# Experts sorted by tokens and run in pairs of 128 and 64 slots, the 64 resting as high and low rows side by side

## The reference, cut to what matters

```python
logits = (xt @ router_w).astype(jnp.float32)          # (256, 8)
top_logit, top_idx = lax.top_k(logits, TOP_K)         # TOP_K = 2
gates = jax.nn.softmax(top_logit, axis=-1)
...
def swiglu(x, w1, w2):
    gate, up = jnp.split(x @ w1, 2, axis=-1)          # w1: 1024 x 5632
    return (jax.nn.silu(gate) * up) @ w2              # w2: 2816 x 1024
...
yb = yb * slot_gate[:, None]
y = jnp.zeros_like(xt).at[slot_tok].add(yb)
```

## Time and profile before

| | us |
|---|---|
| median of 3 runs (1501.88 to 5215.01) | 1502.48 |
| span of the profiled execution | 1499.8 |
| PE busy in it | 1470.4 (98%) |
| DVE busy | 1172.5 (78%) |
| ACT busy | 944.0 (63%) |
| moved from memory | 388.41 MB, mean 259 GB/s |

### The profile page before, as it was taken

The page is one execution under the profiler, slowest core; times in us unless marked ns, Lnnn a source line. Parts: engine busy times, 40 slices in busy tenths (PEclk is TensorE's granted clock), DMA queues, the critical chain, the costliest instruction groups (busy, mean ns, idle before and its releaser), DMA issues.

```text
span 1499.8 us, 21512 instructions
## 1 busy us (share of the span) xinstructions
PE 1470.4 (98%) x8395; PEld 1278.7 (85%) x8395; DVE 1172.5 (78%) x1150; ACT 944.0 (63%) x963; POOL 52.2 (3%) x58
## 2 busy tenths in 40 slices
PE   7999999999999999998999999999999999999997
PEld 7989898999889989897788888888888888888885
DVE  7878655555447878655998988989989899898996
ACT  6655444444437654444777778777787777777774
POOL 0031000000000131000000000000000000000000
PEclk9999999999999999999999999999999999999999
DMA  8443443445546433534799989999999999999994
GB/s 311 141 141 113 168 164 117 169 171 195 181 164 219 141 113 117 193 114 167 282 359 382 347 341 364 352 378 361 340 357 347 380 362 343 361 347 377 365 357 157
DMA packets 54478, 388.41 MB, mean 259 GB/s; under 512 B 6000, under 2 KB 6256, under 8 KB 8176
## 3 DMA queue, kind: packets, MB, share of 16 engines
q1 hardware_dynamic: 53840, 384.98, 68.7%
q10 hardware_dynamic: 544, 2.10, 0.4%
HBM read 386.00 MB, written 1.05 MB: 258 GB/s over the span
## 4 chain that ended last, share of the span: by engine, by line
PE 92%; DVE 3%; DMA 2%; ACT 1%; issue 1%; POOL 0%; SPq 0%; DVEq 0%; ACTq 0%
PE pb L1059 27%; PE pb L1061 27%; PE pb L1060 27%; PE pb L1461 1%; PE pb L1424 1%; PE pb L1207 1%; PE pb L1289 1%; PE pb L1309 1%; DVE xTl L1636 1%; DMA arena<-in_mem 1%; DVE wlo L2177 1%; PE pb L1040 1%; PE pb L1447 0%; PE pb L1448 0%; DMA raw<-in_lin_w 0%
## 5 line engine op out<-in xcount | busy, mean ns | idle before, releaser
L2177 DVE TENSOR_TENSOR wlo<-raw,whi 128x2048 fp32r<-128x2048 f32 x175 | 400.3, 2291 | 47.7 <-ACT whi L961 46.2
L961 ACT ACTIVATE whi<-raw 128x2048 fp32r<-128x2048 f32 x175 | 335.6, 1920 | 131.9 <-PE pb L1061 131.9
L1587 DVE TENSOR_TENSOR wlo<-raw,whi 128x2048 fp32r<-128x2048 f32 (+1 forms) x101 | 226.0, 2246 | 133.2 <-ACT whi L602 133.0
L1059 PE MATMUL pb<-whi,mTh 128*128 128x512 f32 x768 | 305.2, 397 | 1.6 <-DVE wlo L2177 1.6
L1061 PE MATMUL pb<-whi,mTl 128*128 128x512 f32 x768 | 300.1, 391 | 0.0
L602 ACT ACTIVATE whi<-raw 128x2048 fp32r<-128x2048 f32 (+1 forms) x101 | 189.9, 1884 | 172.3 <-PE pb L1061 167.3
L1059 PE MATMUL pb<-xTh,whi 128*128 128x256 f32 x736 | 210.2, 286 | 2.7 <-DVE xTl L1624 1.2
L2177 DVE TENSOR_TENSOR kvXr<-kvX,whi 128x2048 fp32r<-128x2048 f32 x86 | 196.7, 2291 | 19.3 <-ACT whi L961 17.7
L1060 PE MATMUL pb<-xTl,whi 128*128 128x256 f32 x736 | 208.2, 283 | 0.0
L1061 PE MATMUL pb<-xTh,wlo 128*128 128x256 f32 x736 | 208.2, 283 | 0.0
L1060 PE MATMUL pb<-wlo,mTh 128*128 128x512 f32 x528 | 205.6, 389 | 0.0
(11 more groups left out here) (341 smaller groups left out, 2195.4 us busy)
## 6 DMA issues: line engine op xcount, KB each, us to landing
raw<-in_ffn_w SPq DMA_DIRECT2D x209, 1024.0 KB, 4.8
kvX<-in_ffn_w SPq DMA_DIRECT2D x88, 1024.0 KB, 4.9
raw<-in_lin_w SPq DMA_DIRECT2D x64, 1024.0 KB, 4.8
raw<-in_lin_w SPq DMA_DIRECT2D x4, 536.0 KB, 5.6
arena<-in_mem ACTq DMA_DIRECT2D x2, 1024.0 KB, 8.5
h<-in_x SPq DMA_DIRECT2D x1, 1024.0 KB, 4.9
out<-xn SPq DMA_DIRECT2D x2, 512.0 KB, 3.1
consts<-in_con SPq DMA_DIRECT2D x1, 838.0 KB, 13.6
```

What stands on the lines that cost most here:

```text
L961: nc.scalar.activation(whi[:, (MOE0 + c) % HRING, :], xraw_slots[c % XRING], ACT.Copy).then_inc(hi_ready, 1)
L1059: nc.tensor.matmul(o, lh, rh, start=first, stop=False)
L1587: V.tensor_tensor(wlo[:, m % RING, c], raw[:, m % RING, c], whi[:, m % HRING, c].bitcast(F32), ALU.subtract).then_inc(lo_ready, 1)
L2177: V.tensor_tensor(xlo_slots[c % XRING], xraw_slots[c % XRING], whi[:, (MOE0 + c) % HRING, :].bitcast(F32), ALU.subtract).then_inc(lo_ready, 1)
```

## The change

Experts are sorted by their number of tokens and run in four pairs of a full one (H, 128 slots) and a light one (L, 64 slots). The first full one is always expert 0, which needs no sorting; the other seven are ordered by DVE (MAX, MAX_INDEX on 8 x count + index), the three largest become H, the next four L. SP and nobody else needs the ids as registers (`value_load`). For a light expert the 64 high rows and the 64 low rows of the tokens rest side by side as one stationary operand of 128 columns, so a product takes two matmuls (times high weights, times low weights) instead of three, 8 a chunk instead of 12; the upper 64 rows of the result are then added to the lower 64: ACT copies them down (`low_rows`), DVE adds (`lsum`). The two experts of a pair run interleaved by units (a unit: 2 chunks of w1, or 1 of w2; 22 units an expert), L three units behind H. `WHOLE` is empty: every chunk is split. The gate now scales the expert's output where it is split, so both experts of a pair are spread into one sum and added once. The ring of loaded chunks has a seventh slot (`raw6r` in the `arena`). The loops over pairs are unrolled on ACT, DVE, SP and PE. The second pass runs if expert 0 or the largest other has over 128, or the fourth of the others over 64.

```diff
-XRING = 6
+XRING = 7
+PAIRS_E = NE // 2
+UNITS = NF // 2 + W2_CHUNKS
+LAG = 3
+LIGHT = P // 2
+WHOLE = ()
+def turns():
+    total = PAIRS_E * UNITS
+    return [((divmod(a, UNITS) if a < total else None), (divmod(a - LAG, UNITS) if a >= LAG else None))
+            for a in range(total + LAG)]
+STREAM = [(kind, at[0], c) for step in turns() for kind, at in zip("HL", step) if at
+          for c in unit_chunks(at[1])]
...
+        def column(kind, i):
+            return (i - 1) % NE if kind == "H" else NE // 2 - 1 + i
...
             def load_experts(p):
-                with sp.Fori(0, NE // 2) as pair:
-                    for e in range(2):
-                        for c in range(FFN_CHUNKS):
-                            m = e * FFN_CHUNKS + c
-                            sp.wait_ge(w_used, pair * (2 * FFN_CHUNKS) + (moe_chunk(p) + m - XRING + 1))
-                            sp.dma_start(xraw_slots[m % XRING], ffn_w[1 + pair * 2 + e, c]
-                                         ).then_inc(x_loaded[m % XRING], 16)
+                ids = {}
+                for n, (kind, i, c) in enumerate(STREAM):
+                    at = p * NSTREAM + n
+                    if at >= XRING:
+                        sp.wait_ge(w_used, MOE0 + at - XRING + 1)
...
+                    if (kind, i) != ("H", 0) and (kind, i) not in ids:
+                        if len(ids) == 0:
+                            sp.wait_ge(sorted_ok, 1)
+                        q = column(kind, i)
+                        ids[kind, i] = sp.value_load(eid[0:1, q:q + 1].bitcast(U32), min_val=0, max_val=NE - 1)
+                    e = ids.get((kind, i), 0)
+                    slot = landed(p, n)[0]
+                    sp.dma_start(xraw_slots[slot], ffn_w[1 + e, c]).then_inc(x_loaded[slot], 16)
...
+                def first_product(kind, i, j):
...
+                            if kind == "L":
+                                both = xg[:, k, P:2 * P]
+                                nc.tensor.matmul(o, both, w[0][:, kk, :], start=first, stop=False)
+                                mm = nc.tensor.matmul(o, both, w[1][:, kk, :], start=False, stop=last)
...
+                                mm = split_product(o, [xgh[:, k, 0:P], xgHl[:, k, :]],
+                                                   [part[:, kk, :] for part in w], first, last)
+                        mm.then_inc(w_used, 1)
...
+                def turn_light(i, j):
+                    pe.wait_ge(lg_ready, pair_no(p, i, j))
```

More of the change, by code:

```diff
@@ L284, in build @@
+        xlo_slots = [kvXr[:, 0, :], kvXr[:, 1, :]] + [wlo[:, (MOE0 + i) % RING, :] for i in range(RING)] + [
+            over("raw6r", RAW6, CW)]
         raw12 = small_(NT * 12).rearrange("p (t c) -> p t c", c=12)
@@ L923, in experts @@
             def experts(p):
[L924 to L932, removed]
-                        ins.then_inc(xg_hi, 1)
@@ L947, in two_experts @@
[L947 to L989, removed]
+                w = par_("ffn_w", 1)
+                done = [HRING]
+                def splits_through(n):
+                    while done[0] < NSPLIT and SPLIT[done[0] - HRING] <= n:
+                        split_high(p, done[0])
+                        done[0] += 1
@@ L1004, in experts @@
                 return more if p == 0 else None
[L1006 to L1011, removed]
             more = experts(0)
             with act.If(more):
-                for c in range(HRING):
-                    first_chunk(1, c)
+                for i in range(HRING):
+                    split_high(1, i)
                 experts(1)
@@ L1549, in experts @@
                     pe.wait_ge(xn_lo, 2)
-                for phase in range(2):
-                    gather(p * (NE // 2), phase, 6 - 2 * phase)
-                if p == 0:
-                    for pair in range(NE // 2 - 1):
-                        two_experts(pair, False)
-                else:
-                    with pe.Fori(0, NE // 2 - 1) as pair:
-                        two_experts(pair, False)
-                two_experts(NE // 2 - 1, True)
+                gather_first("H")
+                for a, (full, light) in enumerate(turns()):
+                    if full:
+                        i, u = full
+                        if u < NF // 2:
+                            first_product("H", i, u)
+                        else:
+                            second_product("H", i, u - NF // 2).then_inc(w_used, 1)
+                        if 1 <= u <= NF // 2:
+                            turn_hidden(i, u - 1)
+                    if a == 1:
+                        gather_first("L")
+                    if light and not full and light[1] == UNITS - 2:
+                        break
+                    if light:
+                        i, u = light
+                        if u < NF // 2:
+                            first_product("L", i, u)
+                        else:
+                            second_product("L", i, u - NF // 2).then_inc(w_used, 1)
+                        if 1 <= u <= NF // 2:
+                            turn_light(i, u - 1)
+                    if full:
+                        i, u = full
+                        if u in (5, 7) and i:
+                            spread_outputs(i - 1, (u - 5) // 2)
+                        if u == 9:
+                            turn_selections(i)
+                        if u in (15, 18) and i < PAIRS_E - 1:
+                            gather(i + 1, (u - 15) // 3)
@@ new lines, in first_lo_of @@
+            def first_lo_of(p, kind):
+                w = par_("ffn_w", 1)
+                for r in (range(4) if kind == "H" else (4,)):
+                    dve.wait_ge(first_hi, 5 * p + r + 1)
+                    for k in (range(2 * r, 2 * r + 2) if kind == "H" else range(KT)):
+                        if kind == "H":
+                            low, src, s = xgHl, pb[:, 4 + r, (k % 2) * P:(k % 2 + 1) * P], slice(0, P)
+                        else:
+                            low, src, s = xgLl, pb[:, 3, k * LIGHT:(k + 1) * LIGHT], slice(P, XG)
+                        ins = V.scalar_tensor_tensor(out=low[:, k, :], in0=src, scalar=w[:, k:k + 1],
+                                                     in1=xgh[:, k, s].bitcast(F32), op0=ALU.mult, op1=ALU.subtract)
+                    ins.then_inc(first_lo, 1)
@@ new lines, in _ @@
+            select_full([pos[:, t, 0:1] for t in range(NT)]).then_inc(sel_ready, 1)
+            split_low(0, 1)
+            first_lo_of(0, "H")
+            split_low(0, 2)
+            dve.wait_ge(rt_rank, 2)
+            counts = pb[:, 3, 0:NE]
+            iota8 = const("iota")[:, 0:NE]
+            link(V.scalar_tensor_tensor(out=keys[:, 1:NE], in0=counts[:, 1:NE], scalar=float(NE), in1=iota8[:, 1:NE],
+                                        op0=ALU.mult, op1=ALU.add))
+            link(V.max(sorted_keys, keys))
@@ L2153, in add_outputs @@
                         hh = h[:, t, half * 512:(half + 1) * 512]
[L2154 to L2156 removed]
+                        ins = V.tensor_tensor(hh, hh, pb[:, b, :], ALU.add)
                     ins.then_inc(ffn_added, 1)
[L2160 to L2164 removed]
```

698 lines of the change are left out of this document (461 added, 237 removed).

## The result

The changed kernel takes 1481.49 us (median of 4 runs, 1479.66 to 1482.52), before 1502.18. The ratio is 0.9868, with a 95% interval of 0.9853 to 0.9883: 1.3% faster. One of the four executions of the kernel before took 5215 us, and the ratio compares the ordinary ones alone. The forecast was 1457 us, 45 us less; it came to 21 us less. The direction was right, the size was not, and the gain stays under the 2% above which the forecast speaks of faster.

The account below looks back on a forecast made before the run. PE was taken to bound the kernel, with DVE and transfers close behind. Fourth split at 723.6, plus stage 715 and end 15.5, gave span 1454; the median, 2.7 above span, 1457 us; range 1434 to 1490.

Parts of the forecast that it names:

- PE sets the pace before: Main stage of the kernel before: PE busy all the time, 2.92 us a chunk, DVE and transfers close behind.
- Prices: Per pair of experts, costs summed from operation prices: PE 165 us (2.50 a chunk), DVE 174.0 us (2.64 a chunk).
- Transfers: Loading weight chunks in the stage: 2.60 us a chunk taken, between 2.74 at 383 GB/s and 2.49 at 422.
- Rival 1: Transfers in the stage stay slow: time 1481 at 383 GB/s, 1504 at 359 GB/s; chance 0.14.
- The order within a turn: Turns of four, three and two chunks, each priced by its bound (84.6, 46.8, 41.6 us), summing to 179.2 a pair.
- Rival 2: In the stage the chain through DVE, ACT and PE binds: 0.7 us in each of 32 four-chunk turns, 1480; chance 0.10.
- DVE idle over 8%: Sign in the stage: DVE idle this much behind ACT, at a DMA share under 0.97, would show the binding chain.
- Slips: In the stage, 12 us added for turns with output spreading, said to slip by 0.5 to 1 us.
- Start: Before the stage: 29 small DVE operations take 5.7 us uncovered; the fourth split starts near 723.6 instead of 721.95.
- End: Behind the last split: twelve matmuls instead of eighteen, 15.5 us instead of 16.9.
- Rivals 3 and 4: Whole run: a second pass (some 700 us, 2160) or a falling PE clock in the stage; both slower, chance 0.03 each.
- rival 4: PE's clock falls in the stage; at half clock PE alone needs 5 us a chunk; pauses under 1 us; chance 0.03.

Follow-up runs that it names:

- e2: The changed kernel with the light expert's product against the low weights issued twice, 12 matmuls a chunk as before: 1529.61 us.
- e1: The changed kernel with the light expert's gate product transposed, and split by ACT and DVE, one turn later: 1454.13 us.
- e3: The changed kernel with a 0.25 MB transfer beside every third chunk (8.3% more bytes) and without ACT's unused copies into that tile: 1486.08 us.
- e6: The changed kernel with the gather for the first light expert moved into PE's pause ahead of the fourth chunk: 1475.40 us.
- e9: The changed kernel with the light expert's silu and gate product of the turn before moved ahead of the turn's splits: 1521.36 us.
- e4: The changed kernel with the full experts' odd w1 chunks (11 of 66 a pair) unsplit, multiplied in plain float32: 1470.41 us.
- e5: The changed kernel with 24 idle 128x128 matmuls put into PE's pause ahead of the fourth chunk: 1483.63 us.

## Why the forecast was right and wrong, step by step

**PE sets the pace before, and its matmuls are what is saved.** Right: e2 gives back the saving of the changed kernel and 28 us more.

**Prices.** The four-chunk turns came at 10.7 us against 10.6. Row sum 0.673 us (0.68 forecast), gate product 0.410 (0.38 forecast, with the 0.08 taken off), low part 0.276. The gathers, whose price under 256 columns was open, start 0.11 us apart with 192, 128 and 64 columns, as cheap as before, not twice as dear. In e1 the same prices hold in every turn of this kind.

**Transfers.** 2.60 us a chunk was a guess between two bounds. It did not bind: e3 carries 400 GB/s, 2.6 us. Rival 1 falls for the changed kernel. The Trainium skill ("DMA: Bandwidth & Descriptors", section "Bandwidth") puts the limit of memory to one core at about 358 GB/s. It did not hold for this core: e3 moved 400 GB/s over 680 us.

**The order within a turn.** This step failed. It was laid out by hand for the turn of four chunks alone, where everything fits, and the forecast took the other turns as the larger of three loads. Rival 2 named the very wait, the light product behind the splits, but priced it as 0.7 us in the 32 four-chunk turns, at 0.10. There it cost next to nothing. It cost 3.8 to 5.0 us in turn 16 of the pairs two to four and 2.5 in the first, 0.6 in turns 6, 8 and 10, where PE's own list is longer or DVE's too. A chain of fixed length that a turn of 10.6 us hides isn't hidden in one of 5.2. Turn 16 alone makes 15 us of the 23 that the stage was longer. About 5.6 of the 15 are the lower clock behind the pause, and about 9.6 the wait. e1 gets both back. Turn 11 stays at 9.2 in e1 too (8.4 in the last pair), 1.4 and 0.6 us over its load, and turns 0 and 3 stay at 8.5 to 8.8 and 11.0; the cause was not looked for. The sign that the forecast gave for rival 2, DVE idle over 8%, did not appear (6%); what showed it was PE's wait.

**Slips.** The 12 us were meant for turns with spreading, but six such turns at 0.5 to 1 us make 3 to 6; the sum held twice what the argument gave. The turns slipped by 0.7 to 0.9 us, as said, but 0.6 of it was again the wait for the light product, since e1 takes it away. The surplus of 6 us or more hid a part of the miss: that was luck.

**Start.** The 29 small operations took 4.96 us (716.99 to 721.95), not 5.7, and began 0.9 us earlier than forecast, so the fourth split began at 721.95 instead of 723.6. But the gather for the first light expert stands in no term of the forecast. Its 32 matmuls stood in the path, with ACT's and DVE's eight operations each behind them: 6 us by e6.

**End.** 17.7 instead of 15.5. PE waits 1.92 us for the full expert's output split and then spreads it, both ahead of the last light product; the forecast took this as hidden. Behind that wait eight matmuls (from 1459.24 to 1462.64) run at the lower clock, 1.6 us more. In e1 the same wait is 1.50 us, none of them is slow, and the end takes 16.1 us. The order at the end itself was not tried.

**Rivals 3 and 4.** No second pass: the number of transfers is that of before. The clock did fall, not in the whole stage but for a few us at a time, mostly behind pauses of 1.9 to 3.1 us, where rival 4 reckoned with pauses under 1 us: 0.83 from 720 to 740 us, 0.99 over the stage; e1 has 1.00. Counted over the starts it took about 10 us of the changed kernel: 2.9 at the start, 5.6 in turns 16, 1.6 at the end. In turn 16 it follows the pause, since in e1 both are gone; the second stretch at the start has no pause ahead of it, and its cause is open.

## What to carry to other kernels

When work is interleaved in turns of unequal length, lay out the chain between engines for the shortest turn too, not for the longest alone: each engine's load may fit everywhere and a chain still not fit in one. Here one more turn of delay helped a product that passes from engine to engine, and an earlier place in the queues did not: putting it first made its wait everybody's (e9). And while such a chain is in the way, relieving a loaded engine brings less than freeing the chain (11 us in e4, 27 in e1), though e4 also loaded PE.

## What the runs showed of the hardware that I had not expected

A plain float32 matmul stands as two in the rows, each 0.43 us from start to start for 512 columns at a granted clock of 1.00, so four of them cost 3.43 us (e4); reading 0.216 us for 256 columns in the kernel before as the price of a whole one was wrong by two. The matmuls that gather, on rounded copies, cost 0.11 to 0.12 us alike for 64, 128, 192 and 256 columns. In e5 the clock fell in the middle of a stretch of such 64-column matmuls, with PE busy all the time from 715 us on: their starts are 0.11 us apart, then from 732.46 on 0.21, and the granted clock from 730 to 735 us is 0.75. And the same pause can cost differently: behind 2.9 us the clock stayed up in one pair and fell in three, for 7 to 13 matmuls.
